# The feed-forward panels of a two-layer decoder step, multiplied pair by pair in seven block products

## The reference

```
def swiglu(x, w_gu, w_down):
    gate, up = jnp.split(x @ w_gu, 2, axis=-1)
    return (jax.nn.silu(gate) * up) @ w_down
...
        h = h + rmsnorm(mix, g[1])
        h = h + rmsnorm(swiglu(rmsnorm(h, g[2]), w_gu[layer], w_down[layer]), g[3])
```

## Time and profile before

| | |
|---|---|
| median of 3 runs | 2895.53 us (2893.65 to 2897.58) |
| the profiled execution | 2892.26 us |
| its span, first to last instruction | 2890.3 us |
| PE busy | 2764.8 us, 96% of the span |
| DVE, ACT, POOL busy | 1088.2, 904.3, 246.1 us |
| mean granted TensorE clock | 0.985 |

### The profile page before, as it was taken

How to read it: one execution, slowest core, us unless ns; L and a number is a source line. 1 busy time by engine, 2 the same in 40 slices (tenths; PEclk the granted TensorE clock), 3 DMA queues, 4 the chain that set the end, 5 groups by cost and what they waited for, 6 DMA issues and landing times.

```text
span 2890.3 us, 46645 instructions
## 1 busy us (share of the span) xinstructions
PE 2764.8 (96%) x19337; PEld 1815.1 (63%) x19337; DVE 1088.2 (38%) x1874; ACT 904.3 (31%) x1698; POOL 246.1 (9%) x335
## 2 busy tenths in 40 slices
PE   5999899989999999999899999999989999999997
PEld 4666565655666666666566666767646666666664
DVE  4455542326422102224663434344463221122244
ACT  4454432224322112223433232324352221122232
POOL 3000013222000000001200101010100000000021
PEclk8999999999999999999999999999999999999999
DMA  5211269761111211323454333321401111111242
GB/s 189 81 59 39 66 212 325 233 227 37 30 51 51 61 37 46 64 60 111 110 79 55 68 61 69 53 77 54 143 8 52 52 56 48 44 48 49 66 130 80
DMA packets 289245, 244.27 MB, mean 85 GB/s; under 512 B 10805, under 2 KB 254619, under 8 KB 288397
## 3 DMA queue, kind: packets, MB, share of 16 engines
q1 hardware_dynamic: 269788, 168.20, 22.6%
q0 software_dynamic: 19248, 73.10, 7.3%
HBM read 214.45 MB, written 26.81 MB: 83 GB/s over the span
## 4 chain that ended last, share of the span: by engine, by line
PE 89%; DVE 4%; ACT 2%; DMA 2%; issue 2%; SPq 1%; POOL 0%; DVEq 0%; ACTq 0%; POOLq 0%
PE ps L284 72%; PE ps L1496 2%; PE ps L1484 1%; PE ps L1182 1%; PE ps L2062 1%; PE ps L2053 1%; PE ps L1261 1%; PE ps L2031 1%; PE ps L2006 1%; DMA hT<-in_cache_v 1%; PE ps L2045 1%; DVE arena L625 1%; PE ps L1535 1%; DVE hT L629 1%; PE ps L2019 1%
## 5 line engine op out<-in xcount | busy, mean ns | idle before, releaser
L284 PE MATMUL ps<-u,w_split 128*128 128x352 f16 x9936 | 1531.1, 314 | 9.7 <-DVE arena L1146 3.8
L284 PEld LDWEIGHTS ps<-u,w_split 128*128 128x128 f16 x9936 | 969.7, 98 | 531.0 <-issue 26.5
L284 PE MATMUL ps<-arena,w_split 128*128 128x352 f16 x3663 | 562.4, 314 | 3.0 <-DVE w_split L257 1.5
L257 DVE SCALAR_TENSOR_TENSOR w_split<-w_raw,w_split 128x1024 f16<-128x1024 f32 (+2 forms) x205 | 272.8, 1332 | 732.2 <-ACT w_split L244 731.8
L284 PEld LDWEIGHTS ps<-arena,w_split 128*128 128x128 f16 x3663 | 358.0, 98 | 201.4 <-issue 10.9
L244 ACT ACTIVATE w_split<-w_raw 128x1024 f16<-128x1024 f32 (+2 forms) x205 | 230.8, 1127 | 150.7 <-PE ps L284 99.1
L862 ACT ACTIVATE arena<-arena 128x352 f16<-128x352 f32 x132 | 65.5, 496 | 367.6 <-DVE arena L895 367.6
L868 ACT ACTIVATE arena<-ps 128x352 f32<-128x352 f32 x132 | 61.2, 463 | 315.6 <-PE ps L284 315.6
L895 DVE SCALAR_TENSOR_TENSOR arena<-ps,arena 128x352 f32<-128x352 f32 x132 | 69.3, 525 | 190.8 <-PE ps L284 190.1
L561 POOL TENSOR_TENSOR arena<-arena 128x352 f32<-128x352 f32 x9 | 12.7, 1410 | 1361.9 <-ACT arena L552 1353.8
L284 PE MATMUL ps<-arena 128*128 128x352 f16 x657 | 102.7, 316 | 0.0
(11 more groups left out here) (359 smaller groups left out, 2194.7 us busy)
## 6 DMA issues: line engine op xcount, KB each, us to landing
w_raw<-in_w_gu SPq DMA_DIRECT2D x88, 512.0 KB, 3.8
w_raw<-in_w_down SPq DMA_DIRECT2D x58, 704.0 KB, 4.7
w_raw<-in_w_in SPq DMA_DIRECT2D x56, 512.0 KB, 7.1
hT<-in_cache_k SPq DMA_DIRECT2D x64, 256.0 KB, 4.1
hT<-in_cache_k POOLq DMA_DIRECT2D x64, 256.0 KB, 4.5
hT<-in_cache_v SPq DMA_DIRECT2D x64, 256.0 KB, 5.2
hT<-in_cache_v POOLq DMA_DIRECT2D x64, 256.0 KB, 5.5
hT<-in_state_C POOLq DMA_DIRECT2D x32, 256.0 KB, 3.9
```

The costliest lines, as they stand in the source:

```text
L257: dve.scalar_tensor_tensor(split_of(v, 1)[:, 0:kt * n], w_raw[:, v % 2, 0:kt * n], WS, split_of(v, 0)[:, 0:kt * n], ALU.mult, ALU.subtract ...
L284: ins = pe.matmul(ps[0:m, bank, 0:GW], split_of(v, wp)[:, k * w + col * P:k * w + col * P + m], x[:, xp, k0 + k, cols(g)], start=(k == 0 a ...
```

## The change

**Products.** Two neighbouring gate (or up) panels are computed together as a 2 x 2 block product: the 1024 weight rows in two halves of 4 tiles, the two panels, and the tokens in two halves of 528. In Winograd's order of Strassen's form this takes seven block products M1 to M7 in place of eight. Each is 4 row tiles x 3 part products x 2 segments of HW = 264 columns, 24 matmuls (`pe_product`). Panels 3 to 10 of half 0 are computed so (8 pairs, gate and up), and panels 0 to 9 of half 1 (10 pairs): 18 pairs in a layer, 36 in all. Panel 2 of half 0 and panel 10 of half 1 stay as they were, as do the WAVE and all down panels.

**Weight sums.** For each pair both panels are loaded at once as 1 MB, into `w_raw` or into two rows of `arena` by turns. ACT and DVE split A11, A12 and A22; then GpSimd makes the four sums S1 to S4 in place (`pool_ffn`), and ACT and DVE split those. So a pair has seven splits of 512 columns where two panels had two of 1024.

**Token sums.** Four products take sums T1 to T4 of blocks of `u`. Once in a layer GpSimd rebuilds `u` in float32 (eight additions of 1056 columns), and in four jobs, placed at the WAVE's eleventh unit and at three units of panel 2, DVE makes the sums and ACT and DVE split them (`act_t_job`, `dve_t_job`). They take `hT`'s place, so `hT` is now stored to DRAM in boundaries 0, 1 and 2, and read back by GpSimd's queue after a layer's last product. No M6 starts before all four jobs are done.

**Emptying PSUM.** M1, M6, M7 and M4 add up in one pair of banks, and each state is read before the next is added. ACT copies M1, M6 and M7 out, DVE adds (M2, M3, M7), ACT takes silu in SBUF, DVE multiplies, all on 528 columns; the casts cover 1056. The order on PE is M1 of pair p, M4 and M3 of pair p-1, then M2, M6, M5, M7 of pair p.

**The start.** The token tiles are loaded from SP and ACT by turns, gains after them, then the weights of visits 0 and 1, then the rest. PE transposes tiles first; DVE copies them all; ACT only takes squares, then splits visits 0 and 1; the lambda work moves behind the first norm. Five units, not three, consume the first `u` tile by tile.

```diff
+HW = T // 4
+BLOCK = KD // 2 * P
...
+        t_of = hT.rearrange("p k t -> p (k t)").bitcast(F16).rearrange("p (j l k t) -> p j l k t", j=4, l=2, k=KD // 2)
+        T1, T3, T2, T4 = range(4)
...
+        def add_t_job(n, layer, k):
+
+            t_jobs[n] = k
+            t_turn[n] = turns["dve"] + 1
+            turns["dve"] += 2
+            t_free[n] = t_cast.get(layer, 0)
+            cast_of[n, "t"] = cast(), cast()
+            t_cast[layer] = casts["n"]
...
+        USE = {"M1": "A11", "M2": "A12", "M3": "S4", "M4": "A22", "M5": "S1", "M6": "S2", "M7": "S3"}
+
+        def add_products(layer, half_, firsts):
+
+            todo = [(kind, i) for i in firsts for kind in ("gate", "up")]
+            order = []
+            for p in range(len(todo)):
+                order.append((p, "M1"))
+                if p:
+                    order += [(p - 1, "M4"), (p - 1, "M3")]
+                order += [(p, "M2"), (p, "M6"), (p, "M5"), (p, "M7")]
+            order += [(len(todo) - 1, "M4"), (len(todo) - 1, "M3")]
...
+            for p, (kind, i) in enumerate(todo):
+                c0 = (DFF if kind == "up" else 0) + half_ * KF * P + i * P
+                load = add_load(w_cols(w_gu[layer], slice(c0, c0 + 2 * P)), KD, 2 * P, ("rows", "both")[p % 2])
+                if half_ == 0 and p == 0:
+                    chain_before[load] = 3 * (2 * layer) + 2
+                first = len(VISITS)
+                early, behind = (range(8), range(8)) if p < len(todo) - 1 else ((0, 1, 2, 3, 4), (7, 6, 5))
+                when = at[p - 1, "M6"] if p else start - 5
+                for name in ("A11", "A12", "A22"):
+                    add_block(p, name, when, load, behind if name == "A22" else early)
+                base = place["pair"] * 4 + 8 * (layer + 1)
+                place["pair"] += 1
+                pool_jobs[layer].append((load, first, base))
+                when = at[p - 1, "M4"] if p else start - 2
+                for j, name in enumerate(("S1", "S3", "S2", "S4")):
+                    if name == "S4":
+                        when = at[p - 1, "M3"] if p else start + 1
+                    add_block(p, name, when, load, behind if name in ("S3", "S4") else early)
+                    made_turn[len(VISITS) - 1] = base + j + 1
...
+                bank = {"M2": 6, "M5": 4, "M3": 4}.get(name, 2 * (place["pair"] + p & 1))
...
+                if name in ("M1", "M2", "M5"):
+                    events = sorted({holder[b] for b in (bank, bank + 1) if b in holder})
+                else:
+                    events = [at[p, {"M6": "M1", "M7": "M6", "M4": "M7", "M3": "M7"}[name]]]
...
+            WAVE[b] = []
+            for j in range(12):
+                WAVE[b].append(add_ffn_unit(wave[j % 4], j // 4))
+                if j == 10:
+                    add_t_job(WAVE[b][j], layer, 0)
...
+                if half_ == 0:
+                    add_plain(2, (0, 1))
+                    add_products(layer, 0, range(3, KF, 2))
...
+                    add_products(layer, 1, range(0, KF - 1, 2))
+                    place["slot"] = 0
+                    add_plain(KF - 1, (0, 1))
...
+        def pool_save(pool, gg):
+            h_made(pool, gg, KD - 1)
+            pool.dma_start(spill[:, :, cols(gg % 3)], hT[:, :, cols(gg % 3)]).then_inc(spilled, 16)
...
+            if name == "M3":
+                pe.wait_ge(evac["dve"], sum_turn[extra["m7"]])
+            if name == "M2":
+                for a in range(2):
+                    pe.wait_ge(rs_made[a], 3 * (2 * layer) + 3)
+            if name == "M6":
+                pe.wait_ge(hid_ready, t_cast[layer])
+            for s_ in range(2):
+                for k in range(4):
+                    for q, (wp, xp) in enumerate(((0, 0), (0, 1), (1, 0))):
+                        if name in ("M1", "M2", "M3"):
+                            k0, c0 = {"M1": (0, 0), "M2": (4, 0), "M3": (4, T // 2)}[name]
+                            x = u[:, xp, k0 + k, c0 + s_ * HW:c0 + (s_ + 1) * HW]
+                        else:
+                            j = {"M4": T4, "M5": T1, "M6": T2, "M7": T3}[name]
+                            x = t_of[:, j, xp, k, s_ * HW:(s_ + 1) * HW]
+                        ins = pe.matmul(ps[:, bank + s_, 0:HW], split_of(v, wp)[:, k * P:(k + 1) * P], x,
+                                        start=(name in ("M1", "M2", "M5") and k == 0 and q == 0),
+                                        stop=(k == 3 and q == 2), skip_group_check=True)
+            ins.then_inc(unit_done, 1)
...
+            if name in ("M2", "M3"):
+                first = name == "M2"
+                drained(dve, extra["m1" if first else "m6"])
+                dve.tensor_tensor(out, x, keep[not first], ALU.add).then_inc(evac["dve"], 1)
+            if name == "M7":
+                drained(dve, n)
+                dve.tensor_tensor(out, ps[:, 4:6, 0:HW], out, ALU.add).then_inc(evac["dve"], 1)
+            if kind == "up":
+                dve.wait_ge(evac["act"], silu_turn[key, mn])
+                if name != "M4":
+                    dve.wait_ge(evac["dve"], sum_turn[n])
+                    x = out
+                dve.scalar_tensor_tensor(out, x, 1 / WS, silu_of(*mn), ALU.mult, ALU.mult).then_inc(evac["dve"], 1)
+                if name in ("M3", "M4"):
+                    later.append(lambda: dve_low(dve, hid[:, :, i + mn[0], :], arena[:, 21 + mn[0], :], cast_of[n]))
...
+        def act_t_job(act, n):
+
+            layer = VISITS[UNITS[n].visit].role[1]
+            k = t_jobs[n]
+            act.wait_ge(spilled, (48, 144)[layer])
+            for a in range(2):
+                act.wait_ge(evac["dve"], t_turn[n] + a)
+                act.activation(t_of[:, 2 * a:2 * a + 2, 0, k, :], two(19 + a), ACT.Copy).then_inc(hid_hi, 1)
...
+            dve.wait_ge(block_made, 8 * layer + 2 * k + 2 + (len(pool_jobs[0]) * 4 if layer else 0))
+            dve.tensor_tensor(t13, far, near, ALU.subtract).then_inc(evac["dve"], 1)
+            dve.wait_ge(evac["dve"], t_turn[n])
+            dve_links["t"].link(dve.tensor_tensor(t24[:, 0], ahead[:, 1], t13[:, 0], ALU.subtract))
+            dve.tensor_tensor(t24[:, 1], ahead[:, 0], t24[:, 0], ALU.subtract).then_inc(evac["dve"], 1)
+            dve.wait_ge(spilled, (48, 144)[layer])
+            for a in range(2):
+                later.append(lambda a=a: dve_low_t(dve, k, a, cast_of[n, "t"][a]))
...
+        def pool_ffn(pool, layer):
+
+            gg = 3 * (2 * layer) + 2
+            done = 8 * layer + (len(pool_jobs[0]) * 4 if layer else 0)
+            u_made(pool, gg, KD - 1)
+            for j in range(KD):
+                k = j // 2 + j % 2 * (KD // 2)
+                pool.tensor_tensor(arena[:, 11 + k, :], u[:, 0, k, :], u[:, 1, k, :], ALU.add).then_inc(block_made, 1)
+            for load, first, base in pool_jobs[layer]:
+                raw = raw_blocks[LOADS[load].raw == "both"]
+                a11, a12, a21, a22 = (raw[:, 4 * k:4 * k + 4, m, :] for k, m in ((0, 0), (1, 0), (0, 1), (1, 1)))
+                pool.wait_ge(w_ready, first + 3)
+                pool.tensor_tensor(a22, a21, a22, ALU.add).then_inc(block_made, 1)
+                pool.wait_ge(block_made, base + 1)
+                pool.tensor_tensor(a21, a11, a21, ALU.subtract).then_inc(block_made, 1)
+                pool.wait_ge(block_made, base + 2)
+                pool.tensor_tensor(a11, a22, a11, ALU.subtract).then_inc(block_made, 1)
+                pool.wait_ge(block_made, base + 3)
+                pool.tensor_tensor(a12, a12, a11, ALU.subtract).then_inc(block_made, 1)
+            pool.wait_ge(unit_done, max(products_of(layer)) + 1)
+            for g in range(3):
+                pool.dma_start(hT[:, :, cols(g)], spill[:, :, cols(g)]).then_inc(restored, 16)
...
+                if tt % 2 == 0:
+                    sp.dma_start(arena[0:w, tt, 0:D], src).then_inc(x_loaded[tt], 16)
+            sp.dma_start(gains_nat[0:64, :], norms.rearrange("l n (k p) -> (l n k) p", p=P)).then_inc(gain_loaded, 16)
+            sp.dma_start(gains_nat[64:72, :], mh_g1.rearrange("a (k p) -> (a k) p", p=P)).then_inc(gain_loaded, 16)
+            sp.dma_start(gains_nat[72:73, :], subln_g0).then_inc(gain_loaded, 16)
+            sp.dma_start(gains_nat[73:85, :], conv_w0.rearrange("a w (k p) -> (a w k) p", p=P)).then_inc(gain_loaded, 16)
+            sp.dma_start(sc_nat, state_conv.rearrange("a b t c -> (a b t) c")).then_inc(gain_loaded, 16)
+            sp.dma_start(n_rows, state_n.rearrange("a b h (k p) -> (a b h k) p", p=P)).then_inc(gain_loaded, 16)
+            for v in range(2):
+                load_tile(sp, v)
...
+            for tt in range(1, NTT, 2):
+                act.dma_start(arena[0:P, tt, 0:D], x_p[0, tt * P:(tt + 1) * P, :]).then_inc(x_loaded[tt], 16)
...
+            split_hi(act, 0)
+            split_hi(act, 1)
             act_first_norm(act)
+            act.wait_ge(lam_ready, 2)
+            act.activation(lam_e, lam_e, ACT.Exp).then_inc(misc_ev, 1)
...
```

(80 more changed lines are left out.)

417 lines of the change are left out of this document (298 added, 119 removed).

## The result

The changed kernel takes 2817.74 us (median of 4 runs, 2814.27 to 2820.16), the kernel before beside it 2896.56 (4 runs, 2893.65 to 2900.90): ratio 0.9726, 95% interval 0.9709 to 0.9743. The forecast of 2807 was 10.7 us too low, inside its range. The profiled execution took 2817.28 us, 75.0 less than that of before, where the sum in the prediction had 88.7.

The account below looks back on a forecast made before the run. PE was taken as the bound, busy 96% of the span. From the profiled 2892.3 us, less 93.0 (matmuls) and 11.7 (start), plus 12 (token sums) and 4 (seams), gives 2803.6; the median lay 3.3 higher, so 2807, range 2788 to 2850.

Parts of the forecast that it names:

- Matmuls, 112.5 ns and 2.70 us a product, 93.0 us in all: FFN pairs: 264-column matmuls at 112.5 ns, 18.90 us a pair against 21.48, saving 93.0 us over 36 pairs.
- No stall inside a row of pairs: Consecutive product pairs: vector work, all under 18.90 us of PE a pair, makes PE wait nowhere.
- dearer matmuls: Rival, chance 0.05: hidden weight loads stop being hidden; at 120 ns a matmul 45 us more, 2852 us.
- the exclusion as the bound: Rival, chance 0.07: DVE instructions wait for GpSimd additions in every pair, which lasts 23 us; 2955 us in all.
- the lossy rival: Chance 0.18: each pair loses about one GpSimd addition (43 us), token sums 15 us a layer; about 2858, half of it 2832.
- a break-even at 108 us of stalls: In the 0.07 rival: the change loses where a pair lasts over 21.5 us, at 108 us of stalls.
- Token sums, a stall of 6 us a layer: Before each layer's first M6, due at U + 39.8 (U: last low part of `u` ends): 6 us stall, 12 in all.
- The bound of full exclusion, 14 us: Token sums: if DVE and GpSimd work runs one at a time, 54 us less 39.8 gives a 14 us stall.
- the rival without stalls: Chance 0.12: no stalls and the better start, 2789 us.
- Other seams, 4 us: Half ends, at the first down unit and at the S3 and S2 splits: 1 us each, 4 us in all, 0 to 12.
- Spills nothing: Storing `hT` and reading it back cost no time; 5 us a layer if reading back delayed the first down panels.
- Start, -11.7 us: Kernel start: root chain 10.5 us earlier, big matmuls from 35.6 instead of 46.30 us; saves 11.7 us, 8 to 14.

## Why the prediction was nearly right, point by point

- *Matmuls, 112.5 ns and 2.70 us a product, 93.0 us in all*: right, 1632 in 183.61 us in two stretches, the loads 87% busy as worked out. Of the Trainium skill's two rules (TensorE: Matmul & The Clock Gate, Back-to-back issue gap) the isolated gap agrees with this number; the one for streams, an estimate of 99 ns from that page, does not.
- *No stall inside a row of pairs*: right; no wait in the stretches above, and quartering the weight sums changed nothing in those of half 1. The rivals of dearer matmuls and of the exclusion as the bound fell with it, and so did the half of the lossy rival that had each pair lose an addition (43 us). The splits took 0.69 and 0.62 us (0.67 and 0.63 forecast), the copies 0.61. GpSimd was busy for 486.4 us where 454 or more was forecast: the weight sums took 187.6 for 172.8, the additions for `u` 43.4 for 35.2. A slip in the rivals: a break-even at 108 us of stalls doesn't follow from the prediction's terms, 93.0 + 11.7 = 104.7; no other number rests on it.
- *Token sums, a stall of 6 us a layer*: **this is the term that was mis-sized**: 13.1 us in each layer. The mechanism, the place, the releaser and the moment at which M6 is due (U + 39.9, forecast 39.8) were right. Each duration of the queue behind it was short. Job 0 was done at U + 24.7 for 20, job 1 at 31.3 for 26, the A splits at 33.1 for 28, job 2 at 42.2 for 35, job 3 at 48.0 for 41, S2 at 53.0 for 45.5. The first 5 us are the eight additions: 21.7 us, not 17.6, since the one row for a 1056-column addition (2.19 us) was of other operands, and each of the eight DVE instructions with two SBUF inputs beside them takes 0.7 to 2 us longer. The next 2 are job 2, stretched by the weight sums, 3.3 us in the experiment that quartered them. The bound of full exclusion, 14 us, and the lossy rival's 15 were given; the value measured lies next to both, and the rival without stalls fell. It should have been the one taken: DVE was full there (45.43 of 48.57 us), so there was no idle time in which an exclusion could hide. With the additions taken away the gap is 2.5 us, with three plain panels none.
- *Other seams, 4 us*: 4 x 0.79 + 2 x 0.38 = 3.9. The size is right, the place half: I had looked at the down unit and at S3 and S2, and the larger part is M4 behind M7 in a last pair, which has no product between.
- *Spills nothing*: right; no PE gap in 65.80 us beside the reading back.
- *Start, -11.7 us*: 13.6 by the start alone. Copies ended 3 us sooner than forecast and the gains held DVE up less, so the roots came 2.2 us sooner and PE began 3.9 us sooner; of this the slower first matmuls took back a part (216 in 35.17 us, at a granted clock of 0.92, not 32.2; 1 us of it was allowed for). One reading was off too: the trace of before has 115 of these matmuls by 66.20 and 121 by 67.10, so 120 were done some 0.9 us later than the prediction says, which alone makes the term 12.6.
- *Left out*: the clock after the gap. Its first 72 matmuls took 10.77 us, and 9.94 in layer 1, where 72 take 8.26 at full clock: 4.2 us.

Together: gap 26.2 in place of 12, -14.2; clock -4.2; start +1.9; seams 0. That is -16.5 against -13.7 measured (75.0 and 88.7). The 2.8 us over are not attributed; executions of one kernel lie further apart than that.

## What to carry to other kernels

In this kernel the shorter matmuls paid off in proportion, with their weight loads hidden and 87% busy, and vector work on GpSimd was free where DVE was half full. In the one stretch where DVE was full, the gap came out at the bound of full exclusion (13.1 us for 14), not at a value between, and the work handed to GpSimd cost what it cost on DVE. So look first for the stretch in which the vector engine is full, and take the bound there. Then ask first whether what waits can be put behind other work of PE; giving up 10 us of the gain for a later first consumer bought back 26 of gap and 4 of slow clock.
